# Reordering the first stage of a two-block kernel: earlier squares, spread gates and bias tiles, an output projection ahead of a turn, and sums in three steps

## The chip, the cores and the metric

One core of one Trainium2 chip. Time is the device time of one execution in microseconds (us), lower is better. TensorE (PE) multiplies and turns, VectorE (DVE) and ScalarE (ACT) work on rows, GpSimd (POOL) helps them, SyncE (SP) issues the transfers of weights.

## The reference

Two transformer blocks over 256 tokens of width 1024, in float32. The change is in the first half of the first block:

```python
h = rms_norm(x, g_mix)
z = h @ w_in            # fq, fk, fv (512 each), ff (8), dq, dk, dv (512 each), ga, gb (1024 each)
log_f = log_sigmoid(ff + b_fgate);  F = cumsum(log_f)
o_a = softmax(fq fk' / 8 + F[q] - F[k], causal) fv          # 8 heads
o_b = rms_norm((softmax(s1) - lam * softmax(s2)) dv)        # 4 heads, each of two softmaxes
y = sigmoid(ga + b) * (o_a @ w_pa) + sigmoid(gb + b) * (o_b @ w_pb)
x = x + y @ w_o
```

Then come a mixture of 32 experts (two for each token) with 192 MB of weights, and a second block, whose modulation `silu(c) @ w_ada_2 + b_ada_2` is computed in the first stage already, as filling.

## The kernel before

The programs of all compute engines are written from one list, `O1.steps`: Python code adds steps by name, and each engine's function (`first_steps_pe`, and a `first_steps` for each of the vector, scalar and pool programs) goes through the list in its order and does its own part of each step, behind waits on semaphores. So the place of a step in the list is its place in the queue of every engine that has a part in it.

Weights come in chunks of 2 MB through a ring of five slots in SBUF; SP loads a chunk when the chunk before it in its slot is done with. A chunk of the first stage is used in four pieces of 128 x 1024 (ff in one). For exact products each piece is split into a high part, rounded to FP32R on ACT (L1753, step "split"), and a low part, the rest, on DVE (L1199) or, for each piece whose number leaves 3 by 4, on POOL (L2083). There are three buffers for parts, so the split of piece i waits until PE is done with piece i - 3, and `Order.take` adds the split of piece i + 2 just ahead of the use of piece i. A piece costs PE 24 products of 256 columns or 12 of 512. Pieces 0 to 3 are fq, 4 to 7 fk, 8 to 11 fv, 12 ff, 13 to 16 dq, then dk, dv, the gates g0 to g3, pa (41 to 44), pb (45 to 48), wo0 (49 to 52), wo1.

The stage goes like this. SP loads ident, both halves of x, the rows of constants, then fq, fk and small tables. PE does 16 products without use (`warm`), turns the constants (L848), then turns the normed x in four steps "turn1" (L915). ACT squares and scales the first half of x (L1739, L1741), DVE copies the turned constants (L1708) and then squares and scales the second half (L1208, L1202); POOL makes both factors. Then fq, fk, a small product "rel", fv and ff are computed in a row, and "forget" makes the log gates on DVE and ACT.

From there the softmaxes of 16 score tiles are spread over 18 rounds i, with products from the generator `fill_first` between them: pieces of dq, dk, dv and the gates, and for each chunk of w_ada_2 the step "ada" (16 products with the silu of c, spread in SC32 over 32 columns, as the stationary side), a copy to ACC on ACT (L1797) and "ada_sum", which sums ACC's rows on PE. "cumsum" turns the log gates and sums them; between its two parts DVE copies the turned ones to SBUF (L1277). "bf" makes the bias tiles of two heads (DVE L1205 into Bf). Behind bf 3 DVE makes SC32, in the place where negF lay, which the bf products read. Each round adds scores ("qk", for two tiles), "soft" (L1332, ACT L1818), the turn of the probabilities ("p_turn", L921), their product with v, and for the last four heads "diff_mix" (DVE: two reciprocals L1307, L1308, the scaling L1202, the mix L1205), the norm in "diff_out" and "diff_turn" (L1007). In round 16 head 2's diff_turn comes first, then pa's first piece, then p_turn of head 3, then pa's second.

Then pb's four pieces follow, with the sums of y: step "y" multiplies the piece by its gate and adds PA on DVE (L1199, twice), rounds it on ACT (L1862), and takes the rest on DVE (L1199). The last, "x_again", loads x again from ACT's queue. At last y @ w_o: the first two column blocks of y are needed by wo's first piece, the next two by its second, and so on.

## Time and profile before

| | us |
|---|---|
| three runs: lowest, median, highest | 1093.87, 1096.76, 1097.78 |
| the profiled execution | 1091.67 |
| its span, first to last instruction | 1089.9 |
| PE busy | 1013.1 (93%) |
| DVE, ACT, POOL busy | 396.3, 368.8, 133.8 |

The span falls into the first stage (0 to 257 us), routing (to 277), the experts (to 745), a hand-over (to 790) and the second block. A row of the timeline has the start, the duration, engine, line, operation, destination and source, shapes and count, and in brackets how long the engine had been idle and what released it. The granted clock is given as a share of 2.4 GHz; it has the two levels 1.00 and 0.50.

### The profile page before, as it was taken

What the parts mean: (1) busy time and instruction counts of PE and PEld (TensorE: products, weight loads), DVE (VectorE), ACT (ScalarE), POOL (GpSimd) and SP (SyncE); (2) the same over time, 40 slices, a digit from 0 to 9 for tenths busy, and PEclk for the clock granted to TensorE, in tenths of its full rate; (3) what the DMA queues carried; (4) which work ended last, traced back from release to release, by engine and by line L of the source; (5) the groups of instructions that cost most, each with busy time, mean ns of one, the idle gap of its engine ahead of it and who ended that gap; (6) DMA issues with size and microseconds to landing.
All of it is one profiled execution on the core that took longest, in us unless ns stands there. A gap on an engine that the chain in (4) does not pass through costs nothing.

```text
span 1089.9 us, 14867 instructions
## 1 busy us (share of the span) xinstructions
PE 1013.1 (93%) x6333; PEld 711.3 (65%) x6333; DVE 396.3 (36%) x757; ACT 368.8 (34%) x606; POOL 133.8 (12%) x83
## 2 busy tenths in 40 slices
PE   7989999988999999999899989886999999999996
PEld 7978688866444444433334333335998999999995
DVE  3444445554311111111111111214433443783464
ACT  4445555533011111111111101114445554654442
POOL 1111011212000000000000000002312112242122
PEclk8999999999999999999999999998999999999998
DMA  8864466557599999999999999997354544554400
GB/s 297 311 244 169 164 232 235 229 193 309 190 421 419 420 419 419 420 418 421 420 419 420 419 420 419 420 407 283 127 190 165 186 164 164 197 179 158 173 1 39
DMA packets 83003, 307.92 MB, mean 283 GB/s; under 512 B 6607, under 2 KB 11112, under 8 KB 58352
## 3 DMA queue, kind: packets, MB, share of 16 engines
q1 hardware_dynamic: 79144, 302.16, 70.8%
q10 hardware_dynamic: 3784, 4.73, 1.3%
q8 instruction: 51, 0.84, 0.3%
q14 instruction: 24, 0.20, 0.1%
HBM read 305.81 MB, written 2.63 MB: 283 GB/s over the span
## 4 chain that ended last, share of the span: by engine, by line
PE 67%; DMA 13%; DVE 8%; SPq 4%; ACT 4%; issue 2%; POOL 1%; ACTq 0%; POOLq 0%; DVEq 0%
PE bank L738 65%; DMA arena<-in_w 10%; SPq L790 4%; DMA ring<-in_w 2%; DVE arena L1199 2%; DVE arena L1202 2%; DVE wR L1199 2%; DVE arena L1205 1%; ACT wR L1753 1%; PE bank L1148 1%; PE bank L921 1%; ACT arena L1919 1%; POOL wR L2083 0%; POOL small L2071 0%; PE bank L915 0%
## 5 line engine op out<-in xcount | busy, mean ns | idle before, releaser
L738 PE MATMUL bank<-hTR,wR 128*128 128x256 f32 x2520 | 318.5, 288 | 3.6 <-DVE wR L1199 2.1
L738 PEld LDWEIGHTS bank<-hTR,wR 128*128 128x128 f32 x2520 | 310.8, 195 | 7.1 <-issue 6.4
L738 PE MATMUL bank<-ring,arena 128*64 128x512 f32 (+1 forms) x1056 | 230.1, 607 | 10.0 <-DMA ring<-in_w 7.6
L1753 ACT ACTIVATE wR<-ring 128x1024 fp32r<-128x1024 f32 x161 | 168.1, 1053 | 120.1 <-PE bank L738 117.8
L1199 DVE TENSOR_TENSOR wR<-ring,wR 128x1024 fp32r<-128x1024 f32 x121 | 152.2, 1265 | 155.4 <-ACT wR L1753 155.2
L738 PE MATMUL bank<-arena 128*64 128x512 f32 (+7 forms) x778 | 165.3, 533 | 10.2 <-DMA arena<-in_w 7.7
L738 PEld LDWEIGHTS bank<-ring,arena 128*64 128x64 f32 (+1 forms) x1056 | 69.6, 136 | 142.5 <-issue 131.5
L1199 DVE TENSOR_TENSOR arena<-arena,bank 128x256 f32<-128x256 f32 (+1 forms) x36 | 16.0, 450 | 359.5 <-ACT arena L1919 353.9
L2083 POOL TENSOR_TENSOR wR<-ring,wR 128x1024 fp32r<-128x1024 f32 x40 | 97.4, 2434 | 376.6 <-ACT wR L1753 376.6
L1898 ACT ACTIVATE arena<-bank 64x512 f32<-64x512 f32 x64 | 37.9, 592 | 303.4 <-PE bank L738 303.0
L738 PEld LDWEIGHTS bank<-arena 128*64 128x64 f32 (+4 forms) x778 | 64.8, 149 | 96.1 <-issue 80.2
L2071 POOL TENSOR_TENSOR small<-small,mhalf 128x1 f32<-128x1 f32 (+1 forms) x12 | 8.2, 682 | 497.4 <-DVE small L1205 489.9
L1919 ACT ACTIVATE arena<-bank 128x256 f32<-128x256 f32 x32 | 12.3, 384 | 97.7 <-PE bank L738 97.7
L738 PE MATMUL bank<-wR,hTR 128*128 128x512 f32 x192 | 45.3, 393 | 0.0
L738 PEld LDWEIGHTS bank<-wR,hTR 128*128 128x128 f32 x192 | 35.6, 188 | 8.4 <-issue 1.1
L738 PEld LDWEIGHTS bank<-PmR,XShR 128*128 128x128 f32 x128 | 24.1, 188 | 24.0 <-issue 23.5
L738 PE MATMUL bank<-PmR,XShR 128*128 128x256 f32 x128 | 34.9, 307 | 0.1
L738 PE MATMUL bank<-ident 128*128 128x128 f32 x174 | 25.6, 317 | 7.4 <-issue 4.9
L738 PE MATMUL bank<-PmR,XSlR 128*128 128x256 f32 x128 | 31.7, 281 | 0.0
L1202 DVE TENSOR_SCALAR arena<-bank,col 128x256 f32<-128x256 f32 x68 | 29.6, 476 | 5.4 <-PE bank L738 3.7
L738 PEld LDWEIGHTS bank<-ident 128*128 128x128 f32 x174 | 24.8, 231 | 8.3 <-issue 5.6
L738 PE MATMUL bank<-wR,yR 128*128 128x512 f32 x96 | 23.9, 409 | 5.4 <-POOL wR L2083 4.0
(202 smaller groups left out, 847.8 us busy)
## 6 DMA issues: line engine op xcount, KB each, us to landing
ring<-in_w SPq DMA_DIRECT2D x120, 1024.0 KB, 25.1
arena<-in_w SPq DMA_DIRECT2D x72, 1024.0 KB, 25.5
ring<-in_w_in SPq DMA_DIRECT2D x30, 2048.0 KB, 8.5
ring<-in_w_ada SPq DMA_DIRECT2D x6, 2048.0 KB, 7.9
ring<-in_w_o SPq DMA_DIRECT2D x2, 2048.0 KB, 8.4
ring<-in_w_o_attn SPq DMA_DIRECT2D x2, 2048.0 KB, 7.8
ring<-in_w_o_conv SPq DMA_DIRECT2D x2, 2048.0 KB, 7.6
ring<-in_w_out SPq DMA_DIRECT2D x2, 2048.0 KB, 9.1
```

What stands on the lines that cost most here:

```text
L738: return pe.e.matmul(o, l, r, start=start, stop=stop)
L790: e.e.dma_start(to[:, at_:at_ + k * n].rearrange("p (k n) -> p k n", k=k), part).then_inc(landed[nm][0], 16)
L921: last = eng.transpose(banks[u.bank][:, 128 * c:128 * c + 128], P[:, 128 * c:128 * c + 128], ident[:, :])
L1148: last = eng.transpose(banks[x.bank][:, 128 * c:128 * c + 128], Hb[e % 2][:, c:256:2], ident[:, :])
L1199: return eng.tensor_tensor(o, a, b, op)
L1202: return eng.tensor_scalar(o, a, s1, s2, op0) if op1 is None else eng.tensor_scalar(o, a, s1, s2, op0, op1)
L1205: return eng.scalar_tensor_tensor(out=o, in0=a, scalar=s, in1=b, op0=op0, op1=op1)
L1753: eng.activation(h, w, ACT.Copy).then_inc(s_high, 1)
L1898: last = eng.activation(Y[h0:h0 + 64, 512 * h:512 * h + 512], banks[u.bank][64 * h:64 * h + 64, :], ACT.Copy)
L1919: eng.activation(Hb[e % 2], banks[u.bank][:, 0:256], ACT.Silu).then_inc(S["silu"], 1)
L2071: eng.tensor_tensor(o, a, mhalf[:, 0:a.shape[1]], ALU.pow).then_inc(after, 1)
L2083: eng.tensor_tensor(l, pieces[i][1], h.bitcast(F32), ALU.subtract).then_inc(low[i][0], 1)
```

## The change

The order of steps is changed at five places; no arithmetic is.

- **Start.** DVE squares the second half of x ahead of the copy of the constants; 16 warming products become 9 before and 5 behind the turn of the constants. The Silu of c moves from behind turn1 to behind fq.
- **Forget gates, bias tiles.** The turn of the log gates becomes a step of its own, "forget_turn", and one fill step comes between it and "cumsum", one behind "cumsum" and one behind bf 0. In the rounds a bias tile comes behind the first fill step. SC32 is made with bf 1 and lies over Bf's first head.
- **Ada.** For w_ada_2's first four chunks ada_sum comes behind the gates' next piece instead of ahead of it.
- **pa.** In round 16 the rest of the fill and pa's first piece come ahead of head 2's diff_turn.
- **y.** Step "y" is split in y_sum (DVE), y_high (ACT) and y_low (DVE), and these are laid around the pieces of pb; x_again moves to pb's second piece, and the split of piece 51 comes ahead of the last y_high.

```diff
-        SC32 = area(95, 8, 32)
+        SC32 = area(24, 8, 32)
...
-        O1.add("start")
+        PB.use("rows", 7)
         for j2 in range(4):
...
-        PB.use("rows", 7)
-        O1.add("silu_c")
...
         project(O1, "fq", "h1")
+        O1.add("silu_c")
         project(O1, "fk", "h1")
...
             for g in range(4):
-                yield from ada_step(g)
+                b = ada(g)
+                yield
                 for c2 in range(2):
                     u = PB.use((f"g{g}", c2), PR.next())
                     for st in O1.pair(f"g{g}", c2, u, "h1"):
                         O1.add(*st)
                         if st[3] == 0:
+                            if c2 == 0:
+                                ada_sum(g, b)
                             yield
...
             for i in (4, 5):
-                yield from ada_step(i)
+                b = ada(i)
+                yield
+                ada_sum(i, b)
...
         PB.use("zT", 7)
+        O1.add("forget_turn")
+        next(fill)
         PB.use("cum", 7)
         O1.add("cumsum")
-        for _ in range(2):
-            next(fill)
+        next(fill)
         O1.add("rbuf")
         PB.use(("bf", 0), SR.next())
         O1.add("bf", 0)
+        next(fill)
...
                 O1.add("soft", i)
+            if i == 16:
+                for _ in fill:
+                    pass
+                pa_outer(0)
             if late:
...
+            if i < 16:
+                next(fill, None)
             if i < 6 and i % 2 == 0:
                 PB.use(("bf", i // 2 + 1), SR.next())
                 O1.add("bf", i // 2 + 1)
-            if i < 16:
-                next(fill, None)
-            elif i == 16:
-                for _ in fill:
-                    pass
-                pa_outer(0)
...
             done_by(i_, u)
+            if jj == 1:
+                O1.add("x_again")
+            elif jj:
+                O1.add("y_high", jj - 1)
             O1.add("outer", i_, "pb", jj)
             if jj:
-                O1.add("y", jj - 1)
-        O1.add("y", 3)
-        O1.add("x_again")
+                if jj == 1:
+                    O1.add("y_sum", 0)
+                O1.add("y_sum", jj)
+                if jj == 1:
+                    O1.add("y_high", 0)
+                O1.add("y_low", jj - 1)
+        O1.more()
+        O1.add("y_high", 3)
+        O1.add("y_low", 3)
...
-            warm(pe, banks[6], 16)
+            warm(pe, banks[6], 9)
             pe.wait_ge(s_rows, 16)
             eng.transpose(banks[7][:, 0:NROW], VR[0:NROW, :], ident[0:NROW, 0:NROW]).then_inc(full[7], 1)
+            warm(pe, banks[6], 5)
...
-                    if a[0] == 3:
+                    if a[0] == 1:
                         v.wait_ge(s_siluc, 1)
                         ts(SC32, ...)
...
-                elif what == "y":
+                elif what == "y_sum":
                     jj = a[0]
                     u, T = U_["pb", jj], YT[jj % 2]
+                    if jj > 1:
+                        v.wait_ge(s_y, jj - 1)
...
+                elif what == "y_low":
+                    jj = a[0]
                     v.wait_ge(s_yh, jj + 1)
...
+            v.wait_ge(s_x[1], 16)
+            eng.tensor_tensor_reduce(XS1[:, 1, :], XN[:, 1, :], XN[:, 1, :], 1.0, 0.0, ALU.mult, ALU.add,
+                                     ss[:, 1:2]).then_inc(s_sq[1], 1)
             filled(v, U_["rows"])
             eng.tensor_copy(col[:, :], banks[7][:, 0:NROW]).then_inc(U_["rows"].free, 1)
-            v.wait_ge(s_x[1], 16)
-            rms_square(XN[:, 1, :], XS1[:, 1, :], 1, as_is)
+            v.wait_ge(s_rs[1], 1)
+            ts(XS1[:, 1, :], XN[:, 1, :], ss[:, 5:6], None, ALU.mult).then_inc(s_norm[1], 1)
```

## Rows read from the trace of the kernel before

**Rows 1.** Windows: interval, its length, busy us (instructions) by engine, PE clock, DMA share, GB/s

```profile
268.00:277.00 9.00, 6.51 (x53) 5.96 (x52) 6.97 (x39) 1.50 (x2) 0.00 (x0) 1.00 0.12 50
277.00:745.00 468.00, 435.87 (x2154) 180.71 (x2155) 88.37 (x208) 71.48 (x128) 0.00 (x0) 0.99 0.99 409
```

**Rows 2.** Waits of PE, 0 to 277 us: total, times, longest; first row from the groups

```profile
L738 PE MATMUL bank<-wR,yR 128*128 128x512 f32 x96 | 23.9, 409 | 5.4 <-POOL wR L2083 4.0 <-DVE arena L1199 1.4
...
PE bank L915 <- DVE arena L1202: 3.0, 1, 3.0
...
PE bank L738 <- DVE small L1277: 2.4, 1, 2.4
PE bank L1007 <- DVE arena L1202: 2.3, 2, 2.0
PE bank L738 <- issue: 1.7, 1, 1.7
PE bank L738 <- DVE arena L1205: 1.1, 1, 1.1
PE bank L738 <- ACT arena L1797: 1.0, 2, 0.7
```

**Rows 3.** Windows of the six stretches at the lower clock

```profile
12.10:22.30 10.20, 8.46 (x37) 7.69 (x38) 7.24 (x12) 7.42 (x13) 0.00 (x0) 0.50 1.00 333
66.60:70.00 3.40, 3.40 (x13) 1.95 (x13) 1.41 (x3) 0.00 (x0) 0.00 (x0) 0.51 0.91 341
80.40:83.70 3.30, 3.30 (x16) 3.30 (x17) 1.34 (x4) 0.90 (x1) 2.33 (x1) 0.50 0.53 197
114.50:117.90 3.40, 3.40 (x19) 0.94 (x9) 0.00 (x0) 0.60 (x1) 0.00 (x0) 0.50 0.00 0
196.40:199.90 3.50, 3.12 (x15) 3.12 (x16) 3.39 (x11) 0.00 (x0) 2.01 (x1) 0.51 1.01 414
234.00:237.30 3.30, 2.81 (x7) 2.24 (x8) 2.65 (x2) 0.00 (x0) 0.43 (x1) 0.50 0.42 93
```

**Rows 4.** The DMA issued at 2.65 us (us to landing), and ACT's timeline

```profile
ring<-in_w_in SPq DMA_DIRECT2D x1, 2048.0 KB, 10.1
...
14.89 1.06 ACT L1753 ACTIVATE wR<-ring 128x1024 fp32r<-128x1024 f32 x1
...
17.43 1.28 ACT L1766 ACT_TABLE_LOAD   x1
18.72 0.21 ACT L1766 ACTIVATE small<-col 128x8 f32<-128x8 f32 x1
```

**Rows 5.** Timeline, low parts on DVE and POOL around the forget gates

```profile
56.29 1.22 DVE L1199 TENSOR_TENSOR wR<-ring,wR 128x1024 fp32r<-128x1024 f32 x1 [1.92 <-ACT wR L1753]
...
61.72 2.38 POOL L2083 TENSOR_TENSOR wR<-ring,wR 128x1024 fp32r<-128x1024 f32 x1 [10.66 <-ACT wR L1753]
62.62 2.56 DVE L1199 TENSOR_TENSOR wR<-ring,wR 128x1024 fp32r<-128x1024 f32 x1 [1.49 <-ACT wR L1753]
```

**Rows 6.** Timeline, the last ada product, head 2's turn and head 3's mix

```profile
191.06 1.92 PE L738 MATMUL bank<-ring,arena 128*32 128x512 f32 x16
...
196.78 0.69 PE L1007 MATMUL bank<-ident,arena 128*128 128x128 f32 x2 [2.02 <-DVE arena L1202]
...
196.96 1.47 DVE L1202 TENSOR_SCALAR small<-small 128x2 f32<-128x2 f32 x1
...
197.12 4.29 PE L738 MATMUL bank<-oaR,wR 128*128 128x256 f32 x24
...
199.06 0.75 DVE L1205 SCALAR_TENSOR_TENSOR arena<-arena,small 128x128 f32<-128x128 f32 x2
```

**Rows 7.** Timeline, pb's four pieces, a sum of y, wo's last six pieces

```profile
211.62 11.68 PE L738 MATMUL bank<-obR,wR 128*128 128x256 f32 x96
...
228.77 0.69 DVE L1199 TENSOR_TENSOR arena<-arena 128x512 f32<-128x512 f32 x1
...
234.49 17.95 PE L738 MATMUL bank<-wR,yR 128*128 128x512 f32 x72 [4.02 <-POOL wR L2083]
```

More of the change, by code:

```diff
@@ L169, in bass_two_hybrid_blocks @@
         PT = [area(88, 384), area(89.5, 384)]
-        ACC, SC32, abr = area(93, 512), area(95, 8, 32), sm(168, 24)
+        ACC, SC32, abr = area(93, 512), area(24, 8, 32), sm(168, 24)
         TMP = [area(91 + i, 256) for i in range(4)]
@@ L488, in fill_first, with ada @@
             yield
-            def ada_step(i):
+            def ada(i):
                 u = PB.use(("adaw", i), PR.next())
@@ L493, in ada_step, with ada_sum @@
                 O1.loads.release(f"ada{i}")
-                yield
-                PB.use(("ada", i), u.bank)
+                return u.bank
+            def ada_sum(i, bank):
+                PB.use(("ada", i), bank)
                 O1.add("ada_sum", i)
             for g in range(4):
-                yield from ada_step(g)
+                b = ada(g)
+                yield
                 for c2 in range(2):
@@ L941, in first_steps_pe @@
                 mm(pe, banks[u.bank][0:8, 0:384], RB[0:32, :], OH[0:32, :], True, True).then_inc(u.full, 1)
-            elif what == "cumsum":
-                BF = banks[7]
+            elif what == "forget_turn":
                 pe.wait_ge(s_logf, 1)
@@ L946, in first_steps_pe @@
                 for n in range(NT):
-                    last = eng.transpose(BF[:, 8 * n:8 * n + 8], fz[0][:, 128 * n:128 * n + 128], ident[0:8, 0:8])
+                    last = eng.transpose(banks[7][:, 8 * n:8 * n + 8], fz[0][:, 128 * n:128 * n + 128], ident[0:8, 0:8])
                 last.then_inc(U_["zT"].full, 1)
+            elif what == "cumsum":
+                BF = banks[7]
                 may_write(pe, U_["cum"])
@@ L1274, in first_steps @@
                     stt(z, z, 0.0, lz, ALU.min, ALU.subtract).then_inc(s_logf, 1)
-                elif what == "cumsum":
+                elif what == "forget_turn":
                     filled(v, U_["zT"])
                     eng.tensor_copy(lf, banks[7][:, 0:16]).then_inc(U_["zT"].free, 1)
+                elif what == "cumsum":
                     filled(v, U_["cum"])
@@ L1372, in first_steps @@
                     tt(T, T, flat2(PA, 2 * jj), ALU.add).then_inc(s_ysum, 1)
+                elif what == "y_low":
+                    jj = a[0]
                     v.wait_ge(s_yh, jj + 1)
-                    tt(flat2(yR[:, 1], 2 * jj), T, flat2(yR[:, 0], 2 * jj).bitcast(F32), ALU.subtract).then_inc(s_y, 1)
+                    tt(flat2(yR[:, 1], 2 * jj), YT[jj % 2], flat2(yR[:, 0], 2 * jj).bitcast(F32), ALU.subtract).then_inc(s_y, 1)
             def route():
@@ L1856, in first_steps @@
                     last.then_inc(s_gate, 1)
-                elif what == "y":
+                elif what == "y_high":
                     jj = a[0]
```

## The prediction

> **What bounds the kernel now.** I read the stages first. From 277 to 745 us the DMA engines are full (share 0.99, 409 GB/s): the expert stage runs at the rate at which its weights arrive. From 268 to 277 us, just ahead of it, they are nearly idle (0.12), so all eight weight buffers are full before the first expert begins [rows 1]. The change touches only what lies ahead of 257 us. A microsecond saved there starts the expert stage, and with it the release of every buffer, a microsecond sooner, and so the whole rest. It is lost only if transfers were under way at the hand-over, which they aren't.
>
> In the first stage TensorE (PE) is the bound: it is busy nearly throughout, and the view of the waits gives what it lacks in few pieces [rows 2]: in the output product 4.0 us for a low part on GpSimd (POOL) and 1.4 for a sum on VectorE (DVE), 3.0 for the second normed half of x, 2.4 for the copy L1277 of the turned forget gates, 2.3 for the row of head 2 (2.0) and head 3 (0.3), 1.7 with no releaser, 1.1 for the bias tile, 1.0 for ACC (0.7 its longest). The third view is the granted clock. Behind each of the long waits lies a stretch at 0.50, the 1.2 GHz level, with PE at work: 12.1 to 22.3, 66.6 to 70.0, 80.4 to 83.7, 114.5 to 117.9, 196.4 to 199.9, 234.0 to 237.3 [rows 3]. Work in them takes twice as long, so a stretch of 3.4 us costs 1.7 us on top of the wait that came before it.
>
> **The change, part by part.** "Saved" is PE time on the path that sets the end.
>
> **Start.** DVE squares x's second half before it copies the turned constants, and 16 warming products become 9 and 5. The wait of 3.0 us [rows 2] can go. What is late next: ScalarE's (ACT's) high part of the first weight piece at 14.89 waits for the weights too, and their transfer, issued at 2.65 us, takes 10.1 us [rows 4], so it lands at 12.75. The first product can come sooner by 14.89 - 12.75 = 2.1 us, not 3.0. Bounds: 0 and 3.0. PE is still without work between the transposes and the weights, so I leave the slow stretch from 12.1 to 22.3 as it is; a clock that didn't fall would give 2.5 us more (of its 10.2 us some 5 are products of the projection, and they would take half the time). Shorter warming costs nothing: it runs in a wait for DMA. The Silu (a table load of 1.28 and 0.21 [rows 4]) moves behind the first projection, ahead of the high part of piece 6. That part may start when piece 3 is done and is needed two pieces later, 2 x 2.9 = 5.8 us (pb: four pieces in 11.68 [rows 7]); it needs 1.06 on ACT and at most 2.38, POOL's time for a low part [rows 5]. 1.06 + 2.38 + 1.49 = 4.9 is under 5.8: 0, or 1 us if the cover is thinner.
> The Trainium skill (ScalarE: Activation LUTs, What ACT_TABLE_LOAD costs) puts a switch of tables at about 2.66 us with its drain. The trace has the Silu start 1.29 us after the load started; by the page's figure the sum would lose 0 to 0.5 us here.
>
> **Forget gates and bias tiles.** Before, PE turns the gates and then waits 2.4 us for L1277, which stands in DVE's queue behind the low part L1199 of 62.62 (2.56 us, where one alone takes 1.22) and an eviction, so until 65.9. Now piece 15 runs between turning and sum. Its low part is POOL's, ready at 61.72 + 2.38 = 64.1 [rows 5]; PE has turned the gates by 65.9 - 2.4 = 63.5. So about 0.6 to 0.8 of the 2.4 stays: 1.6 saved. The copy comes at 65.9 as before, under piece 15, which runs until 67. In the loop, the bias tile comes between two fill steps; the 1.1 us for the first one's sums (PE now has piece 17 between tile and scores) goes too. With waits of at most 0.8 left, both slow stretches at 66.6 and 80.4 should go: 3.4 and 3.3 us of full work, 3.3 saved. Together 1.6 + 1.1 + 3.3 = 6.0. Bounds: 1.5 (the clock falls anyway, and half the waits come back) and 6.5.
>
> **SC32 and the ada sums.** SC32 was made behind the last bias tile (and in its place over negF, it had to be); PE waits 1.7 us for it, the wait with no releaser, and the stretch at 114.5 follows. It is now made behind tile 1, over the first bias row, which head 0's softmax has already used, many steps ahead of the first ada product. 1.7 + 1.7 saved. The column sums come a whole weight piece (2.9 us) behind the ACT copy they need, so one wait of 0.7 of the 1.0 [rows 2] goes as well. Sum 4.1; bounds 2.4 and 4.4.
>
> **pa ahead of head 2's turn.** This is the part I think goes against the change. Removed: the wait of 2.0 and the slow stretch at 196.4 (1.7). But the fill was also brought forward by a step, so an ada product of 1.92 us [rows 6] that lay between the last scores and the last heads' turns now lies ahead of the scores, and the softmax chain of the last heads has 1.9 us less cover, and 2.9 more from pa: the wait for head 2's turn becomes 2.0 + 1.9 - 2.9 = 1.0. And behind head 2's row, DVE still has to mix head 3: scaling from 196.96 (1.47, stalled) to the end of L1205 at 199.06 + 0.75 = 199.8, 3.0 us after the turn at 196.78. That was hidden by pa's first piece (4.29 us). With pa in front, only the turn itself (0.3) is left to cover it: 2.7 us of new wait at L921, with pa 1 queued behind. The new waits, 3.7 us in 4, should bring their own slow stretch, now over pa 1: 1.7. Net 3.7 - 3.7 - 1.7 = -1.7. Bounds: -5 (the stretch is twice as long) and +3.7 (DVE isn't stalled and the scores aren't late).
>
> **y in three steps.** Gone: the wait of 4.0 for the low part of piece 51, whose high part was queued on ACT behind y 3 and two DMA issues, the wait of 1.4 (a bank freed late), and the slow stretch at 234.0 (1.6) [rows 2, 3, 7]. The issues of x move to pb 1, where ACT has nothing that PE waits for. What is late next: DVE has in each pb step of 2.9 us one low part (1.22 [rows 5]) and three sums of 0.69 [rows 7], 3.3 us in all, so it falls behind by 0.4 a step from the end of pb's first piece at 211.62 + 2.92 = 214.5. I walk its queue: y 0 sent at 220.5, y 1 at 223.8, y 2 at 227.1, y 3 at 227.9. PE needs them at 223.2, 226.0, 228.8 and 231.6. All are hidden, y 2 by 1.7 us. Saved 4.0 + 1.4 + 1.6 = 7.0; bounds 3 (y 2 or piece 51 is late, the clock falls again) and 7.
> A stall to weigh here: DVE's scaling of 0.2 us took 1.47 [rows 6] and L1199 took 2.56 [rows 5], both while POOL's low part ran. POOL's low part of piece 51 now lies over y 3's second sum; so stalled, y 2 is sent at 228.7, by 0.1 us not late.
> The Trainium skill (SBUF — State Buffer, SBUF: two separate sides) has this as an exclusive lock on a port pair between DVE and GpSimd; the trace agrees with its two rows. It speaks against putting DVE's sums and POOL's part side by side, and leaves the sum as it is.
>
> **Sum.** 2.1 + 0 + 6.0 + 4.1 - 1.7 + 7.0 = 17.5 us. The profiled execution took 1091.67 us around a span of 1089.9; by it, the changed kernel's would take 1074.2. It was faster than all three runs shown, whose median is 1096.76, so I take the sum off the median: 1079.
>
> **Rivals.**
> One: **the tail and the clock give half back**. The slow stretches go with PE's pauses, and pauses of 0.8 at 63.5 and 1.0 and 2.7 at the heads' turns remain. If two of the five stretches that I strike stay (3.3) and the tail costs 5, gain 17.5 - 3.3 - 3.3 = 11: 1086. For it: rows 3 have a stretch behind each long wait. Against: none lies behind the wait of 0.7 for ACC.
> Two: **the expert weights swallow it**, no change, 1096. It needs the DMA engines at work at the hand-over; their 0.12 speaks against it.
> Three, **slower**: the clock goes down at the new wait for head 3's mix and stays down. In 12.1 to 22.3 it stayed at 0.50 for 10.2 us although PE was busy for 8.46 [rows 3]. At 1.2 GHz the seven pieces from pa 1 to pb 3 cost 7 x 2.9 = 20 us more, and wo's six further ones (72 products, 17.95 [rows 7], 2.75 each at full clock) and two before them 22. With 1.6 less from y: 17.5 - 20 - 22 - 1.6 = -26, 1123. Slower than before begins when it stays down for six more pieces.
> Four: **the start keeps its clock**, and no new stall comes at the tail: 17.5 + 2.5 + 4 = 24, 1073.
> That the change doesn't do what it says (SC32 early, but ada's weights late) costs at most SC32's 3.4 us: inside the range.
>
> **Numbers.** Forecast 0.72, one 0.14, two 0.05, three 0.03, four 0.06. A measurement of this kernel can tell about 0.5%, 5.5 us. Faster by more: 0.72 + 0.14 + 0.06 = 0.92; within: 0.05; slower: 0.03. The range takes in the forecast's bounds, where one or two terms fail, most of rival one and the runs' own spread: 1072 to 1086.
>
> **What the changed profile would show.** Right: the first product at about 15.2; no wait on L1277 over 1 us; clock 1.00 between 24 and 190 us; no wait with no releaser at the first ada product; wo without a gap over 1 us, its last product at about 235 instead of 252.4. And at the tail a wait at L921 of 2 to 3 us ahead of pa 1. Wrong: no such wait (I was too dark), first product still at 17.3, y 2 as the releaser of wo's third piece, or an expert stage longer than 468 us.

## The result and the profile after

The changed kernel takes 1077.32 us (median of 4 runs, 1073.11 to 1078.87), the kernel before 1095.32 (4 runs, 1091.95 to 1097.78) on the same chip: a ratio of 0.9843, 95% interval 0.9818 to 0.9867. The forecast was 1079. The profiled executions are 1078.87 after and 1091.67 before, a difference of 12.8 us, while the medians differ by 18.0. The one after is the slowest of its four runs, the one before is faster than all four of its own, so the 12.8 understates the gain. Where those 5 us lie has a part of its own below.

The diff shifts the lines: L738, L915, L921, L1007 and L1202 of before are L756, L934, L940, L1027 and L1222 after; L1199 is L1219, L1205 is L1225, L2083 is L2111.

First the waits of PE over the first stage and the routing behind it (0 to 262 us; total, times, longest), all from 0.5 us up. Against them stand [rows 2].

```profile
PE bank L934 <- ACT arena L1769: 3.8, 2, 2.6
PE bank L940 <- DVE arena L1225: 2.6, 1, 2.6
PE bank L756 <- DVE wR L1219: 2.6, 1, 2.6
PE bank L756 <- DMA ident<-in_k_ident: 2.6, 1, 2.6
PE bank L756 <- DVE arena L1219: 2.5, 1, 2.5
PE bank L934 <- DVE hTR L1225: 1.1, 1, 1.1
PE bank L756 <- POOL wR L2111: 0.7, 1, 0.7
PE bank L1027 <- DVE arena L1222: 0.6, 1, 0.6
PE bank L1063 <- DVE arena L1414: 0.5, 1, 0.5
```

Gone are L1277's 2.4, the 3.0 ahead of x's second turn, the 1.7 with no releaser, the 2.0 ahead of head 2's turn and both stalls of the output product. New are 0.7 for a low part on POOL (piece 15) and 2.6 at L940, the turn of head 3's row. The 2.6 for wR of L1219 is the wait for the first weight piece; the 2.5 for arena of L1219 and the longest of L1769 lie behind the stage. The timeline shows the stage's marks:

```profile
15.46 24.75 PE L756 MATMUL bank<-hTR,wR 128*128 128x256 f32 x192 [2.55 <-DVE wR L1219]
...
61.66 3.10 PE L756 MATMUL bank<-hTR,wR 128*128 128x256 f32 x24 [0.72 <-POOL wR L2111]
...
184.57 0.44 PE L1027 MATMUL bank<-ident,arena 128*128 128x128 f32 x2 [0.59 <-DVE arena L1222]
184.69 1.53 DVE L1222 TENSOR_SCALAR small<-small 128x2 f32<-128x2 f32 x1
187.63 0.90 PE L940 MATMUL bank<-ident,arena 128*128 128x128 f32 x3 [2.63 <-DVE arena L1225]
188.19 5.40 PE L756 MATMUL bank<-oaR,wR 128*128 128x256 f32 x24
...
200.06 11.68 PE L756 MATMUL bank<-obR,wR 128*128 128x256 f32 x96
211.58 21.95 PE L756 MATMUL bank<-wR,yR 128*128 128x512 f32 x96
213.55 2.32 DVE L1219 TENSOR_TENSOR arena<-arena 128x512 f32<-128x512 f32 x1
```

The projection starts at 15.46 instead of 17.35. pb starts at 200.06 instead of 211.62 [rows 7], and the output product runs through in 21.95 us; before it took 29.3, to 252.44. It ends at 211.58 + 21.95 = 233.53: **18.9 us earlier**, where the working had 17.5. The row at 188.19 is pa 1, on which the clock falls: 24 products in 5.40 us. The last row is y 3's second sum (a like one took 0.69 before [rows 7]), beside POOL's low part, which runs from 212.92 to 215.32; no one waits for it.

The granted clock (windows: interval, length, busy us and instructions of PE, PEld, DVE, ACT, POOL, clock, DMA share, GB/s):

```profile
15.90:19.30 3.40, 3.40 (x18) 3.40 (x17) 3.25 (x5) 1.51 (x2) 0.00 (x0) 0.50 1.02 322
24.00:186.70 162.70, 159.46 (x1183) 135.17 (x1181) 74.95 (x197) 87.77 (x185) 26.59 (x16) 1.00 0.73 259
186.80:190.20 3.40, 2.56 (x12) 2.57 (x13) 1.63 (x4) 1.61 (x2) 0.00 (x0) 0.50 0.04 17
190.20:193.60 3.40, 3.40 (x19) 3.40 (x18) 1.79 (x2) 2.26 (x4) 0.00 (x0) 0.53 0.00 0
193.70:233.50 39.80, 39.80 (x250) 36.03 (x249) 25.07 (x32) 18.75 (x27) 8.31 (x6) 1.00 0.62 229
```

Of the six stretches at the 1.2 GHz level [rows 3] one at the start is left, 3.4 us instead of 10.2, and one at the tail, now 6.8 us instead of 3.5. The other four are gone.

**The same stage, profiled again.** A later kernel, e11 below, differs from the changed one by a line in the expert stage alone. Its first stage is the changed kernel's, with waits of 2.39 and 2.63 us at the two places where it had 2.55 and 2.63, and there the clock did not fall. Three rows of its timeline, and its window from 12 us to the stage's end:

```profile
15.05 23.26 PE L756 MATMUL bank<-hTR,wR 128*128 128x256 f32 x192 [2.39 <-DVE wR L1220]
...
185.74 0.55 PE L940 MATMUL bank<-ident,arena 128*128 128x128 f32 x3 [2.63 <-DVE arena L1226]
...
207.67 21.95 PE L756 MATMUL bank<-wR,yR 128*128 128x512 f32 x96
...
12.00:229.60 217.60, 210.71 (x1520) 182.26 (x1521) 110.16 (x244) 116.75 (x225) 37.84 (x23) 1.00 0.70 252
```

The output product ends at 229.62, 3.9 us before 233.53: 0.4 from the first product, 1.5 up to head 3's turn and 2.0 from there to pb. So the waits repeat within 0.2 us, but whether a stretch at the lower clock follows them differs between executions, and one profile's end of the stage carries up to 3.9 us of that.

**Where the profiled execution gives some back.** I followed three marks: the output product's last end, the first SP issue of the second block's weights, 5.7 and 5.8 us behind the last of the experts' (before at 711.84, after at 694.08), and the last scatter (before at 745.97, after at 732.56). Earlier by: 18.9, 17.8, 13.4. So the expert stage passes the gain on, up to its last 50 us, and loses 4.35 us there. The windows of before, then of after:

```profile
711.80:745.90 34.10, 26.43 (x128) 11.62 (x125) 7.88 (x19) 6.98 (x12) 0.00 (x0) 1.00 1.03 401
```

```profile
694.10:732.50 38.40, 30.73 (x144) 12.94 (x141) 7.88 (x19) 6.99 (x12) 0.00 (x0) 0.99 1.03 398
664.10:684.10 20.00, 16.96 (x68) 6.46 (x64) 3.55 (x9) 4.08 (x7) 0.00 (x0) 0.83 1.02 421
684.10:704.10 20.00, 17.73 (x91) 6.48 (x90) 2.39 (x8) 3.28 (x6) 0.00 (x0) 0.91 1.01 419
```

From that issue to the last scatter it is 34.1 us before and 38.5 after. Just ahead of that issue the clock of the changed kernel falls (0.83 and 0.91), and the same 32 products of an expert, behind the same wait, show what that does. Timeline, before and after:

```profile
690.24 7.09 PE L738 MATMUL bank<-arena 128*64 128x512 f32 x32 [1.32 <-DMA arena<-in_w]
```

```profile
672.29 9.94 PE L756 MATMUL bank<-arena 128*64 128x512 f32 x32 [1.31 <-DMA arena<-in_w]
```

The waits aren't new; the clock fell behind one and not behind the other. What PE was late by moves behind the mark: 144 products lie there instead of 128. Over twelve further kernels below the distance takes two main values: 33.7 to 35.2 us in seven, 38.3 to 38.7 in four, 37.0 in one. The clock sorts them: all five kernels with 38.3 or more, the changed one among them, have a stretch of 6.8 us at the lower clock that starts 22.5 to 22.8 us ahead of the mark, and a second of 3.4 by 12 us behind it; the six with 34.5 or less, the kernel before among them, have none between 45 us ahead and 33 behind; the three with 35.1, 35.2 and 37.0 have one of 3.4 in that span. It isn't tied to any one edit of the first stage, and it moves the total by 4 us.

So I compare the parts of the change by the output product's end in the profile ("wo end", 233.53 for the changed kernel), and the total only for sums of parts. With one profile of each kernel, though, a wo end is only good to the 3.9 us above; a smaller difference is read from the waits. That a kernel's runs differ by up to 8.4 us (e7) fits the same cause: the changed kernel's four had mean clocks of 0.973, 0.973, 0.977 and 0.980 at 1078.87, 1078.15, 1076.49 and 1073.11 us.

### The profile page after: what moved, and what is told of

Same layout as the page of the kernel before. It is cut to its first block, busy times and chain, and to the rows that moved or that the text cites. A ratio compares the mean times of both kernels' runs of the same rounds, so it can differ in the third digit from the quotient of the medians.

```text
span 1077.1 us, 14861 instructions
## 1 busy us (share of the span) xinstructions
PE 1009.5 (94%) x6329; PEld 707.1 (66%) x6329; DVE 394.1 (37%) x757; ACT 368.6 (34%) x606; POOL 133.9 (12%) x83
## 3 DMA queue, kind: packets, MB, share of 16 engines
HBM read 305.81 MB, written 2.63 MB: 286 GB/s over the span
## 4 chain that ended last, share of the span: by engine, by line
PE 71%; DMA 11%; DVE 8%; SPq 4%; ACT 3%; issue 2%; POOL 1%; POOLq 0%; ACTq 0%; DVEq 0%
PE bank L756 69%; DMA arena<-in_w 5%; DMA ring<-in_w 5%; SPq L808 4%; DVE arena L1222 2%; DVE arena L1219 2%; DVE arena L1225 1%; DVE wR L1219 1%; DMA ring<-in_w_in 1%; PE bank L1168 1%; ACT wR L1781 1%; ACT arena L1947 1%; PE bank L940 1%; POOL wR L2111 0%; PE bank L934 0%
## 5 line engine op out<-in xcount | busy, mean ns | idle before, releaser
L756 PE MATMUL bank<-hTR,wR 128*128 128x256 f32 x2520 | 316.4, 286 | 6.4 <-DVE wR L1219 3.6
L756 PEld LDWEIGHTS bank<-hTR,wR 128*128 128x128 f32 x2520 | 307.8, 193 | 11.4 <-issue 10.1
L756 PE MATMUL bank<-ring,arena 128*64 128x512 f32 (+1 forms) x1056 | 232.0, 609 | 7.9 <-DMA ring<-in_w 7.8
L1219 DVE TENSOR_TENSOR wR<-ring,wR 128x1024 fp32r<-128x1024 f32 x121 | 151.1, 1255 | 136.9 <-ACT wR L1781 136.6
L756 PE MATMUL bank<-arena 128*64 128x512 f32 (+7 forms) x778 | 167.5, 540 | 7.4 <-DMA arena<-in_w 6.5
L756 PEld LDWEIGHTS bank<-ring,arena 128*64 128x64 f32 (+1 forms) x1056 | 70.0, 137 | 142.6 <-issue 131.7
L1219 DVE TENSOR_TENSOR arena<-arena,bank 128x256 f32<-128x256 f32 (+1 forms) x36 | 16.0, 450 | 364.1 <-ACT arena L1947 358.5
L2111 POOL TENSOR_TENSOR wR<-ring,wR 128x1024 fp32r<-128x1024 f32 x40 | 97.3, 2433 | 354.2 <-ACT wR L1781 354.2
L756 PEld LDWEIGHTS bank<-arena 128*64 128x64 f32 (+4 forms) x778 | 65.1, 151 | 94.1 <-issue 82.2
L756 PE MATMUL bank<-wR,hTR 128*128 128x512 f32 x192 | 45.3, 393 | 0.0
L756 PEld LDWEIGHTS bank<-wR,hTR 128*128 128x128 f32 x192 | 35.6, 188 | 8.3 <-issue 1.0
L756 PEld LDWEIGHTS bank<-PmR,XShR 128*128 128x128 f32 x128 | 24.9, 194 | 23.8 <-issue 23.5
L756 PE MATMUL bank<-PmR,XShR 128*128 128x256 f32 x128 | 35.9, 312 | 0.1
L756 PE MATMUL bank<-PmR,XSlR 128*128 128x256 f32 x128 | 32.5, 286 | 0.0
L1222 DVE TENSOR_SCALAR arena<-bank,col 128x256 f32<-128x256 f32 x68 | 29.9, 477 | 6.3 <-PE bank L756 4.2
L756 PE MATMUL bank<-ident 128*128 128x128 f32 x170 | 24.5, 311 | 8.0 <-issue 5.5
L756 PEld LDWEIGHTS bank<-ident 128*128 128x128 f32 x170 | 23.6, 225 | 8.6 <-issue 5.9
L1219 DVE TENSOR_TENSOR arena<-bank,arena 128x512 f32<-128x512 f32 (+2 forms) x30 | 19.6, 665 | 20.5 <-PE bank L756 17.3
```

Source lines behind the costliest of these rows:

```text
L756: return pe.e.matmul(o, l, r, start=start, stop=stop)
L1219: return eng.tensor_tensor(o, a, b, op)
L1222: return eng.tensor_scalar(o, a, s1, s2, op0) if op1 is None else eng.tensor_scalar(o, a, s1, s2, op0, op1)
L2111: eng.tensor_tensor(l, pieces[i][1], h.bitcast(F32), ALU.subtract).then_inc(low[i][0], 1)
```

## The experiments

All kernels are the changed one with one edit, unless said. "Before" is the kernel before on the same chip.

**Each part undone.** The start: 16 warming products at once, constants' copy ahead of the square, Silu ahead of the projection.

```diff
-        project(O1, "fq", "h1")
         O1.add("silu_c")
+        project(O1, "fq", "h1")
```

> The changed kernel with its start alone put back (16 warming products, copy of the constants ahead of DVE's square, Silu ahead of the first projection). My theory: the start is worth what the first weight transfer leaves, so the first product moves from 15.5 back to 17.3 us, and the wo products end at 235.3 to 237 us instead of 233.4 (1.9 from the weights, up to 1.7 more from the clock, whose slow stretch behind the start was 3.4 us in the changed kernel and over 5 us of projection before). Rival: the start was hidden, nothing moves after 40 us. Time about 1079 to 1080.

Measured: first product at 16.48 (+1.0, the theory had 1.8), wo end 235.07 (+1.5); 1076.33 us (1072.43 to 1080.23), ratio to before 0.9829 (0.9776 to 0.9881). The wait of 3.0 ahead of x's second turn is back. The rest of the 1.5 is the clock's: the stretch at the start was 6.8 us long here (14.1 to 20.9). In the twelve kernels with the changed start the first product comes between 14.96 and 15.54. The start is worth 1.0 us or a little more beside the other parts, and the total can't show it.

The forget gates and bias tiles:

```diff
         O1.add("forget_turn")
-        next(fill)
         PB.use("cum", 7)
         O1.add("cumsum")
         next(fill)
+        next(fill)
...
         O1.add("bf", 0)
-        next(fill)
...
-            if i < 16:
-                next(fill, None)
             if i < 6 and i % 2 == 0:
                 PB.use(("bf", i // 2 + 1), SR.next())
                 O1.add("bf", i // 2 + 1)
+            if i < 16:
+                next(fill, None)
```

> The changed kernel with the fill steps alone put back: forget_turn directly ahead of cumsum, four fill steps ahead of the rounds, bias tiles ahead of the round's first fill step; SC32 stays early. My theory: the wait for L1277 (2.4 us), that for the bias tile (about 1) and two slow stretches of 3.4 us come back: 6 us. But the tail has its ada product of 1.9 us as cover again, so the wait ahead of head 3's turn falls from 2.6 to about 0.7 and that for head 2's goes: 2.5 us, and the slow stretch of 6.8 us may go as well (3.4). Net: the wo products end 0 to 4 us later than 233.4. Rival, that the tail has nothing to do with the number of fill steps: they end 6 us later, with the 2.6 us wait still there.

Measured: wo end 240.89 (+7.4); 1086.09 us (1084.51 to 1088.2, 7 runs), ratio 0.9921 (0.9897 to 0.9946). The 2.4 for the copy and the 1.1 for the sums are back, and so are two slow stretches, each twice as long as before's [rows 3]:

```profile
63.90:70.20 6.30, 6.30 (x26) 4.85 (x27) 1.63 (x3) 0.00 (x0) 0.00 (x0) 0.50 0.95 329
...
76.90:83.70 6.80, 6.49 (x25) 4.93 (x26) 3.42 (x10) 1.93 (x5) 2.37 (x1) 0.51 0.53 197
```

At the tail the wait of L939 (L940 of the changed kernel) went only from 2.6 to 1.9, against my theory's 0.7, and that of 0.6 for head 2's turn is gone: 3.2 became 1.9, so neither theory nor rival has it right. The stretch there was 3.4 us instead of 6.8. The part is worth the working's 6.0 or more; the 1.4 beyond it is less than what the clock moves, and both stretches of 6.3 and 6.8 follow waits that were followed by 3.4 and 3.3 before.

y in three steps, put back in four, with x's issues behind it:

```diff
-            if jj == 1:
-                O1.add("x_again")
-            elif jj:
-                O1.add("y_high", jj - 1)
             O1.add("outer", i_, "pb", jj)
             if jj:
-                if jj == 1:
-                    O1.add("y_sum", 0)
-                O1.add("y_sum", jj)
...
+                for st in ("y_sum", "y_high", "y_low"):
+                    O1.add(st, jj - 1)
+        for st in ("y_sum", "y_high", "y_low"):
+            O1.add(st, 3)
+        O1.add("x_again")
```

> The changed kernel with y alone put back (three sums of one block directly behind each other, issues of x behind the last, split of piece 51 behind them). Theory: waits of 4.0 and 1.4 us and a slow stretch (1.6) come back, the wo products end at 240.4 instead of 233.4, the 96 wo products take 29.3 instead of 22.0 us. Rival: part of it was the POOL low part lying badly only in the kernel before, then under 5 us. Time about 1084.

Measured: wo end 239.68 (+6.15), 1079.52 us (1075.66 to 1080.57), ratio 0.986 (0.9817 to 0.9904). Timeline of the output product:

```profile
210.28 1.55 PE L748 MATMUL bank<-wR,yR 128*128 128x512 f32 x6
213.21 4.40 PE L748 MATMUL bank<-wR,yR 128*128 128x512 f32 x18 [1.38 <-DVE arena L1211]
221.54 18.14 PE L748 MATMUL bank<-wR,yR 128*128 128x512 f32 x72 [3.93 <-POOL wR L2103]
```

Both stalls of [rows 2, 7] return: 239.68 - 210.28 = 29.4 us for the 96 products against 21.95. That is 7.45 later; wo end moved by 6.15, mainly because the stretch ahead of it at the tail was 3.4 us long here and 6.8 in the changed kernel.

pa's first piece back behind head 2's turn:

```diff
             if late:
...
+            if i == 16:
+                for _ in fill:
+                    pass
+                pa_outer(0)
```

> The changed kernel with pa's first piece put back behind head 2's turn. My theory: the wait for head 2's turn becomes 2.0 + 1.9 = 3.6 to 3.9 us, and pa's piece, at the lower clock, covers head 3's mix, so the wait ahead of its turn goes; the sum of waits is about what it is now (3.2), the slow stretch about the same: the wo products end within 1.5 us of 233.4. Moving pa's piece was worth nothing. Rival: moving it saved a wait of 2 us and a slow stretch, then they end about 3 to 4 us later.

Measured: wo end 234.65 (+1.1), 1073.94 us (1072.53 to 1078.48), ratio 0.9832 (0.9788 to 0.9876).

```profile
185.03 0.69 PE L1027 MATMUL bank<-ident,arena 128*128 128x128 f32 x2 [3.46 <-DVE arena L1222]
185.37 5.47 PE L756 MATMUL bank<-oaR,wR 128*128 128x256 f32 x24
```

The wait is now 3.46 us and in front of head 2's turn, and the slow stretch lies over pa 0. With 0.3 at head 3's last turn the tail waits 3.8 us instead of 3.2. pa ahead trades one wait for another of nearly the size and is worth 0.6 us in waits; the rest of the 1.1 can't be told from the clock, whose stretch at the start was 6.8 us here instead of 3.4. The median is 3.4 us below the changed kernel's, on another chip and with overlapping intervals, so the total doesn't show the part at all.

SC32 can't be put back alone: with the fill a step further on, the first ada product would stand ahead of the last bias tile, behind which SC32 was made, and wait for ever. So it was undone on top of the forget part (e2) and is read against that kernel; apart from it, it wasn't tried.

```diff
-        ACC, SC32, abr = area(93, 512), area(24, 8, 32), sm(168, 24)
+        ACC, SC32, abr = area(93, 512), area(95, 8, 32), sm(168, 24)
...
-                    if a[0] == 1:
+                    if a[0] == 3:
```

> As e2, and SC32 made behind the last bias tile again, in its old place. Theory: against e2 the wait with no releaser (1.7 us) ahead of the first ada product comes back, and behind it a slow stretch of 3.4 us (1.7): the wo products end 3.4 us later than in e2. Rival: the wait returns without a slow stretch, 1.7 us.

Measured: wo end 244.04, 3.15 us behind e2's; one run, 1088.26 us.

```profile
113.89 3.08 PE L755 MATMUL bank<-ring,arena 128*32 128x512 f32 x16 [1.73 <-issue]
```

The wait with no releaser is back, and the 16 products behind it take 3.08 us where they take 1.92 at full clock [rows 6]. Together: 1.5 + 7.4 + 3.15 + 1.1 + 6.15 = 19.3 us, against the measured 18.9. Each term carries the clock's scatter, so that they agree so well is partly luck. The move of ada_sum wasn't undone by itself in any run.

**Why the tail has that wait.** My working had it as cover lost: an ada product that moved ahead of the scores. One fill step less ahead of the rounds puts it back:

```diff
         O1.add("bf", 0)
-        next(fill)
```

> The changed kernel with one fill step less ahead of the rounds (the one behind bf 0), so that the last two ada products come one step later, behind the last scores. Theory of the tail's cover: the waits for head 2's turn (0.6) and ahead of head 3's (2.6) shrink by the 1.9 us of an ada product, to about 1.3 in all; in return the scores of round 0 wait for bf 0's sums again (about 1 us). Wo's end between 231 and 233.4, lower if the slow stretch of 6.8 us goes or halves. Rival, that the wait ahead of head 3's turn hangs on DVE's chain alone (POOL's stall of 1.5 us) and not on PE's cover: it stays at 2.6.

Measured: wo end 233.51, no difference; one run, 1076.41 us. The waits of 1.1 and 0.9 are back. At the tail the one for head 2's turn is gone and the one of head 3 falls from 2.63 to 1.93: 3.2 became 1.9, as in e2. Timeline:

```profile
179.18 3.55 PE L755 MATMUL bank<-ring,arena 128*32 128x512 f32 x16
182.78 0.60 ACT L1824 ACTIVATE arena<-bank 128x512 f32<-128x512 f32 x1 [4.26 <-PE bank L755]
183.28 0.39 ACT L1845 ACTIVATE arena<-arena,small 128x128 f32<-128x128 f32 x1
189.62 0.55 PE L939 MATMUL bank<-ident,arena 128*128 128x128 f32 x3 [1.93 <-DVE arena L1224]
```

ACT's copy of the last ada product (182.78, idle 4.26 ahead of it) stands in ACT's queue ahead of the last exponentials (from 183.28), so the softmax chain waits for that product too. Here it ran at the lower clock. In e2 the same product runs at full clock:

```profile
187.20 1.92 PE L755 MATMUL bank<-ring,arena 128*32 128x512 f32 x16
...
189.69 0.39 ACT L1845 ACTIVATE arena<-arena,small 128x128 f32<-128x128 f32 x1
```

DVE had done its part for these exponentials at 188.23, and they start at 189.69: of the product's 1.92 us the chain is 1.46 longer, and only 0.5 is cover. Another 1.05 is the 8 products of ada_sum, which come behind the scores with it. Both together, 1.5, are near the 1.3 us by which the waits shrank. In the changed kernel the copy (178.64) is done long before the last exponentials (181.33). So the cover theory holds in direction, with 1.3 us instead of 1.9; and the rival, a wait that stays at 2.6, fails. Wo's end says nothing here: the early waits cost 2.0 more, and the clock's stretch was 3.4 us instead of 6.8.

**Cover from work that isn't on the chain.** pa 1 ahead of head 3's turn, pa 2 and 3 a place forward each:

```diff
                 O1.add("diff_turn", h)
+            if i == 16:
+                pa_outer(1)
...
                 O1.add("evict", "pa", 0)
-                pa_outer(1)
+                pa_outer(2)
         O1.add("gate", 1)
         O1.add("evict", "pa", 1)
-        pa_outer(2)
+        pa_outer(3)
...
         O1.add("evict", "pa", 2)
-        pa_outer(3)
```

> The changed kernel with pa's second piece ahead of head 3's turn, its third ahead of head 3's product with v and its fourth ahead of head 3's last turn. Theory: the wait of 2.6 us ahead of head 3's turn is covered by pa 1 (2.9 us), and with it go both halves of the slow stretch (3.4 us): wo's end 5 to 6 us earlier, 227.5 to 228.5, time about 1071. Rival: what was late moves on to pb, which needs head 3's turned rows, with a wait of 2 us or more there, and only 3 to 4 us are won.

Measured: wo end 230.04 (3.5 earlier), 1073.12 us (1068.63 to 1076.99), ratio 0.9795 (0.976 to 0.983).

```profile
187.69 0.50 PE L941 MATMUL bank<-ident,arena 128*128 128x128 f32 x3
...
197.55 10.70 PE L757 MATMUL bank<-obR,wR 128*128 128x256 f32 x87 [0.71 <-DVE obR L1226]
```

The wait and the slow stretch are gone (the clock is 1.00 from 184 to 196); 0.7 and 0.3 us of waits come up at pb, below the rival's 2 us, though the sum is in the rival's 3 to 4. What of the 3.5 is the wait itself shows against e11, where the clock held without this edit: e10 and e12 below, which have the edit and clock 1.00 too, end at 228.52 and 228.48 instead of 229.62, 1.1 us earlier although their first product comes 0.3 later. So pa 1 as cover is worth 1.4 us, and the rest is the clock.

**The clock by itself.** No step moves; PE multiplies the identity while it would wait:

```diff
+                if a[0] > 1:
+                    warm(pe, banks[2], 2 if a[0] == 2 else 6)
...
+                if of == "diff" and h == 3:
+                    emptied(pe, U_["s", 14])
+                    emptied(pe, U_["s", 15])
+                    warm(pe, banks[2], 6)
```

> The changed kernel with products that nobody uses laid into two waits: 2 and 6 behind the last steps of turn1, 6 ahead of the wait for head 3's mix (0.42 us each). No wait is taken away. Theory: the clock falls because PE pauses. With the pauses filled, the slow stretches at 15.9 to 19.3 and 186.8 to 193.6 go while the first useful products start where they did; wo's end 1.7 + 3.4 us earlier less 0.5 of lateness: about 229. Rival: the clock falls for the kind of work (few columns, turns), then the stretches stay and wo's end is at 233.4 or later.

Measured: wo end 229.55 (4.0 earlier); one run, 1067.31 us. The 12 added products ahead of head 3's turn took 1.50 us (each call of `warm` shows as two), and the windows show both stretches gone, with that wait still at 1.28:

```profile
12.00:19.30 7.30, 6.33 (x52) 6.17 (x53) 6.23 (x10) 5.59 (x9) 0.05 (x1) 1.00 1.02 349
183.00:193.60 10.60, 9.01 (x76) 8.62 (x75) 6.67 (x13) 7.32 (x15) 2.62 (x3) 1.00 0.27 90
```

The first product comes 0.5 us sooner (14.96) and no wait of use is gone, so most of the 4 us is the clock's: the slow stretches are a cost of their own beside the waits. That the added products are what held the clock, this run alone doesn't show, since e11 has none of them in this stage, kept its clock too and ends at 229.62. The count over all profiles speaks for them. At the start, ten of the eleven profiles without them have a stretch at the lower clock, and none of the three with them (e8, e10, e12). At the tail, eight of ten with an uncovered wait of 1.3 us or more have one behind it (not e6 and e11); the one with the wait filled and the three with pa 1 as cover have none.

**DVE's stall in head 3's chain.** Low part 43 goes to DVE, and 42 to POOL in its place, so that POOL is idle while DVE mixes:

```diff
         def on_pool(i):
+            if i in (42, 43):
+                return i == 42
```

> The changed kernel with one pair of low parts swapped: piece 43's (pa's third) on DVE, piece 42's on POOL. Theory: POOL's part of 2.34 us no longer lies over DVE's scaling for head 3's mix, so that scaling falls from 1.53 to about 0.25 us and the wait ahead of head 3's turn from 2.6 to 1.3 us. Rival: the scaling is long for another reason and the wait stays at 2.6.

Measured: wo end 232.59 (0.9 earlier); one run, 1070.45 us.

```profile
186.09 0.23 DVE L1224 TENSOR_SCALAR small<-small 128x2 f32<-128x2 f32 x1
...
187.74 0.55 PE L942 MATMUL bank<-ident,arena 128*128 128x128 f32 x3 [1.33 <-DVE arena L1227]
```

The scaling takes 0.23 us instead of 1.53, and the wait falls by the same 1.3. The 0.9 of wo's end is less than the clock's scatter; the two rows are what shows the effect.

**Together, and the experts' clock.** The two edits of e7 and of e8's start:

> pa's second piece ahead of head 3's turn, and unused products in the pause before the first weights (2 and 6). Theory: both add up, the start's slow stretch goes (1.7) and the tail's as in the run with pa two ahead: wo's end at 228 to 228.5 us, first stage 24 us shorter than before the change. Time 1068 to 1075, depending on the 4.3 us of the next run. Rival: they overlap, wo's end at 229.5 or later.

Measured: wo end 228.52 (5.0 earlier), 1070.29 us (1068.41 to 1072.22), ratio 0.9784 (0.9754 to 0.9814), just outside the changed kernel's interval (0.9818 to 0.9867).

Four warming products in each of the last four experts, of the changed kernel:

```diff
                 may_write(pe, sp)
+                warm(pe, banks[sp.bank], 4)
```

> The changed kernel with 4 unused products ahead of the wait in each of the last four experts' spread step (a pause of 1.7 to 1.8 us; 1.7 us of products). My theory of the scatter: in about half of the executions one or two slow stretches fall into the last 50 us of the expert stage, where PE no longer waits for weights, and cost 4.3 us (34 against 38.4 us from the last issue of expert weights to the last scatter). With the pauses filled, that distance is 34 to 35 us in the profile, and the median of the runs is 2 to 4 us lower than the changed kernel's 1077.3. Rival: the 4.3 us come from the transfers, then the median stays and the distance can be 38.

Measured: 1074.08 us (1069.34 to 1076.96, 6 runs), ratio 0.9825 (0.9801 to 0.985). In the profile the distance (from the mark above, which lies 5.8 us behind the last issue of expert weights) is 33.7 us and the clock holds:

```profile
664.10:684.10 20.00, 17.40 (x103) 8.73 (x104) 5.02 (x15) 1.57 (x3) 0.00 (x0) 1.00 1.01 419
684.10:724.00 39.90, 34.17 (x168) 15.41 (x164) 8.19 (x21) 6.98 (x12) 0.00 (x0) 1.00 1.02 402
```

The median is 3.2 us lower than the changed kernel's, but on another chip; by the ratios it is 2 us, the intervals overlap, and the six runs spread over 7.6 us. The kernel before and five of the ten without this edit reach such a distance too: it fits the theory and doesn't prove it. This is also the profile whose first stage, with no edit there, ends at 229.62.

All three edits:

> All three: pa two ahead, unused products at the start and in the last experts. Theory: 5 us in the first stage and 2 to 4 in the experts below the changed kernel: median 1069 to 1071, wo's end at 228 to 228.5, last issue to last scatter 34 to 35 us. Rival: the two savings don't add, median above 1073.

Measured: wo end 228.48, 1067.99 us (1067.72 to 1068.77, 5 runs), ratio 0.9769 (0.9746 to 0.9793). The median is below the theory's 1069 to 1071. This beats both kernels; by the ratios, which take out the difference of the chips, it is 8 us below the changed one. Its runs spread over 1.05 us, the changed kernel's over 5.8. The clock still fell once in the expert stage (3.4 us, 32 us behind the mark; 0.95 in the second row).

```profile
658.07:688.07 30.00, 27.41 (x152) 12.43 (x150) 5.94 (x17) 4.47 (x8) 0.00 (x0) 1.00 1.01 419
688.07:723.20 35.13, 29.73 (x143) 14.46 (x140) 7.88 (x19) 6.98 (x12) 0.00 (x0) 0.95 1.02 400
```

## Why the prediction held, and where its steps didn't

The total, the range and most of the signs came out: the first product (15.46 for 15.2), L1277, SC32 without a wait, clock 1.00 from 24 to 186.7, the output product without a gap, its last end at 233.53 for about 235, the new wait ahead of pa 1 at 2.63 for 2.7. That weights are resident before the first expert [rows 1] carried the gain over 460 us: 18.9 us became 17.8. That the sum came within 1.4 us of the profile and 0.5 of the medians' difference is partly luck: the same stage gained 18.9 us in one profile and 22.8 in another, as the clock fell or held. By step:

- **Start**, 2.1: the first product came 1.9 sooner, limited by the weights' landing as argued. "I leave the slow stretch as it is" was wrong in the good direction: it shrank from 10.2 to 3.4 us, and was absent in e11. Undone beside the other parts, the start is worth 1.0 us in the first product and 1.5 at wo's end.
- **Silu**, 0: held. The trace after has the table load at 29.35 and the Silu at 30.64, and PE waits for no weight piece there. The Trainium skill (ScalarE: Activation LUTs, What ACT_TABLE_LOAD costs) has about 2.66 us with the drain; here the load's start and the Silu are 1.29 us apart again, so the measurement decides.
- **Forget gates and bias tiles**, 6.0: 7.4 by its undoing. The wait left for POOL's part was 0.72, inside my 0.6 to 0.8, and both slow stretches went; e2 and e5 brought them back at twice the length. Behind the same waits they were 3.4 and 3.3 us long before, so the 1.4 is no sure error of the size. The undone kernel also has an ACC wait of 0.9 and an L1352 wait of 0.3, which the working had counted elsewhere or not at all.
- **SC32**, 4.1 with the ACC wait: 3.15 for SC32 alone against 3.4 of the working. The ACC wait is in the forget part's 7.4, so the two together, 10.55, stand against 10.1, closer than the clock's scatter can vouch for.
- **pa ahead and the tail**, -1.7: the size of the new wait at L940 was right, and 0.6 for head 2's turn instead of 1.0. The slow stretch was twice as long as mine, 6.8 us, which is what the lower bound named, and in e11 it didn't come at all. Between the two profiles it is worth 2.0 us, where half its busy 5.96 us would be 3.0. New 0.6 + 2.6 + 2.0 = 5.2, removed 2.0 + 1.6 = 3.6: -1.6, as forecast, and about 0 where the clock holds. **One reason was mis-sized.** "The softmax chain of the last heads has 1.9 us less cover" is 1.3 by e2 and e6, because the chain itself waits for the ada product through ACT's queue. And "the part I think goes against the change" mixes two things: the fill step brought forward lost the 1.3, while pa's move gained 0.6 in waits (e4), since without it head 2's turn would wait 3.46. What makes head 3's wait so long is DVE's stall beside POOL, 1.3 of the 2.6 (e9), as the working had it.
- **y**, 7.0: 6.15 by its undoing, 29.3 - 21.95 = 7.35 between the profiles. y 3's sum was stalled (2.32 against 0.69 [rows 7]) and stayed hidden, as the working had it.

Of the rivals, one (tail and clock) names what happened at the tail but not its size; two and three did not occur; four did in part at the start. One forecast sign appeared though its cause didn't: the expert stage took over 468 us in the profile. Not transfers under way at its start, but the clock towards its end did that, a cost the working did not have. It had called the stage bound by its weights throughout. In the stretch behind the mark PE is busy for 30.73 us after and 26.43 before, 4.3 more, about the loss, while the DMA share is 1.03 in both. So I read PE's time for the last experts as being on the path there. The sorting of all fourteen profiles by their stretches supports it; e11's edit, meant to test it, can't decide it alone.

## What to carry to other kernels

Before you count a product as cover for a chain, look whether its result is evicted by the engine that runs the chain: if it stands ahead in that queue, it lengthens the chain (here by 1.46 of its 1.92 us). After each wait of PE read the granted clock of the next microseconds: the wait of 2.6 us was followed by a stretch that cost 2.0 more in one execution and by none in another. Compare small parts by the waits they change, which repeat from profile to profile, and then by a mark just behind them; even that mark moved by 3.9 us between two profiles of one and the same stage, so one profile of each kernel doesn't rank edits of 1 us.

## What the runs showed that I had not expected

**The clock before its first change.** The warming products at the very start of the changed kernel:

```profile
2.55 3.73 PE L756 MATMUL bank<-ident 128*128 128x128 f32 x18 [2.55 <-DMA ident<-in_k_ident]
...
6.79 1.30 PE L756 MATMUL bank<-ident 128*128 128x128 f32 x10
```

18 take 3.73 us (0.21 each), the next 10 take 1.30 (0.13 each), while the granted clock is shown as 1.00 for both stretches. The view's value ahead of its first change isn't what the products show.

**A small spread with all pauses filled.** With pauses filled at the start and in the experts and pa 1 as cover at the tail, the spread of runs was 1.05 us (5 runs) instead of 5.8 (4 runs); with the stage's edits alone (e10) it was 3.8, with the experts' alone (e11) 7.6. Each of these is a handful of runs, so that the filled pauses make the spread small is likely and not shown.

**A stall for a tiny operation.** DVE's scaling of two columns took 1.53 us beside POOL's low part and 0.23 without it. The Trainium skill (SBUF — State Buffer, SBUF: two separate sides) describes an exclusive lock on a pair of ports that the two engines share, held for a whole instruction; the trace agrees: the scaling ends at 186.22 and POOL's low part at 186.19, and without it beside the scaling the 1.53 us are 0.23 (e9).
